# A two-layer diffusion step in fp32: norm rows split by the column factor alone, token factor and shift at eviction, and the low part of the probabilities as the values' last product

## What is computed

```
def rmsnorm(x, g):
    xf = x.astype(F32)
    y = xf * lax.rsqrt(jnp.mean(xf * xf, axis=-1, keepdims=True) + EPS)
    return (y * g.astype(F32)).astype(x.dtype)
...
        sh1, sc1, g1, sh2, sc2, g2 = jnp.split(jax.nn.silu(cond) @ P['mod_w'][i] + P['mod_b'][i],
                                               MOD_CHUNKS, axis=-1)
        h = rmsnorm(x, P['norm1_g'][i]) * (1 + sc1) + sh1
...
        x = x + g1 * y
        h = rmsnorm(x, P['norm2_g'][i]) * (1 + sc2) + sh2
        x = x + g2 * (jnp.square(jax.nn.relu(h @ P['mlp_w1'][i])) @ P['mlp_w2'][i])
```

## Time and profile before

| | us |
|---|---|
| median of 3 runs | 3153.99 |
| lowest, highest | 3151.72, 3156.88 |
| the profiled execution, its own time | 3155.11 |
| span of its trace | 3153.0 |
| granted TensorE clock over the span | 0.968 of full |

### The profile page before, as it was taken

The page is one execution under the profiler, slowest core; times in us unless marked ns, Lnnn a source line. Parts: engine busy times, 40 slices in busy tenths (PEclk is TensorE's granted clock), DMA queues, the critical chain, the costliest instruction groups (busy, mean ns, idle before and its releaser), DMA issues.

```text
span 3153.0 us, 43418 instructions
## 1 busy us (share of the span) xinstructions
PE 3011.7 (96%) x17065; PEld 2884.9 (91%) x17065; DVE 1491.0 (47%) x1825; ACT 1001.6 (32%) x1439; POOL 904.0 (29%) x573
## 2 busy tenths in 40 slices
PE   7999998999999999888999999998989999999999
PEld 7999998999999999787778888786989999999999
DVE  8445546456445554744566655566442222222222
ACT  3111213111111122323777677776222111121111
POOL 0221121112212121122665556666212112222111
PEclk7999998999999999897999999999989999999999
DMA  5222220222212221120000000000201111111112
GB/s 202 96 80 80 80 100 27 81 80 81 70 61 80 80 73 60 53 82 6 8 7 7 2 7 5 8 7 1 100 27 47 41 40 40 47 40 41 40 45 80
DMA packets 45539, 166.69 MB, mean 53 GB/s; under 512 B 5793, under 2 KB 7457, under 8 KB 45217
## 3 DMA queue, kind: packets, MB, share of 16 engines
q1 hardware_dynamic: 44912, 160.89, 15.0%
q10 hardware_dynamic: 560, 4.87, 0.4%
HBM read 156.15 MB, written 9.58 MB: 53 GB/s over the span
## 4 chain that ended last, share of the span: by engine, by line
PE 53%; issue 30%; POOL 14%; DVE 2%; ACT 1%; POOLq 0%; DVEq 0%; ACTq 0%
PE ps L907 52%; POOL p_lo L505 10%; POOL w_lo L489 2%; DVE x L1466 0%; POOL rot L516 0%; POOL q_tok L520 0%; DVE ps L1382 0%; POOL rot L514 0%; PE ps L1002 0%; PE ps L1212 0%; ACT tmp L592 0%; PE ps L996 0%; DVE tmp L1406 0%; POOLq L504 0%; DVE sums L1801 0%
## 5 line engine op out<-in xcount | busy, mean ns | idle before, releaser
L489 POOL TENSOR_TENSOR w_lo<-w_raw,w_hi 128x1024 fp32r<-128x1024 f32 (+2 forms) x190 | 465.2, 2449 | 1884.3 <-ACT w_hi L585 1884.3
L907 PE MATMUL ps<-h_hi,w_hi 128*128 128x384 f32 x2640 | 606.8, 337 | 37.7 <-DVE h_lo L1447 20.2
L907 PE MATMUL ps<-h_lo,w_hi 128*128 128x384 f32 x2640 | 603.3, 336 | 0.0
L907 PE MATMUL ps<-h_hi,w_lo 128*128 128x384 f32 x2640 | 602.6, 336 | 0.0
L907 PEld LDWEIGHTS ps<-h_hi,w_hi 128*128 128x128 f32 x2640 | 473.7, 190 | 42.4 <-issue 29.8
L585 ACT ACTIVATE w_hi<-w_raw 128x1024 fp32r<-128x1024 f32 (+2 forms) x190 | 194.7, 1025 | 956.7 <-PE ps L907 860.9
L907 PEld LDWEIGHTS ps<-h_lo,w_hi 128*128 128x128 f32 x2640 | 474.3, 189 | 0.0
L907 PEld LDWEIGHTS ps<-h_hi,w_lo 128*128 128x128 f32 x2640 | 473.6, 189 | 0.0
L505 POOL TENSOR_TENSOR p_lo<-p,p_hi 128x512 fp32r<-128x512 f32 (+1 forms) x304 | 389.8, 1294 | 257.2 <-ACT p_hi L830 253.3
L1466 DVE SCALAR_TENSOR_TENSOR x<-ps,mod,x 128x256 f32<-128x256 f32 (+5 forms) x432 | 240.2, 612 | 457.9 <-PE ps L907 456.9
L907 PE MATMUL ps<-hid_hi,w_hi 128*128 128x384 f32 x1536 | 348.8, 334 | 0.5 <-DVE x L1466 0.5
(11 more groups left out here) (142 smaller groups left out, 3551.4 us busy)
## 6 DMA issues: line engine op xcount, KB each, us to landing
w_raw<-in_wall_dram SPq DMA_DIRECT2D x174, 512.0 KB, 3.7
mod_raw<-in_mod_rows_dram SPq DMA_DIRECT2D x80, 512.0 KB, 3.6
x<-in_x_t_dram SPq DMA_DIRECT2D x8, 576.0 KB, 8.4
x_spill<-x ACTq DMA_DIRECT2D x1, 4608.0 KB, 13.8
x<-x_spill SPq DMA_DIRECT2D x1, 4608.0 KB, 13.5
out_dram<-x SPq DMA_DIRECT2D x8, 576.0 KB, 2.8
mod_shift<-in_mod_cols_dram SPq DMA_DIRECT2D x8, 512.0 KB, 14.5
mod_scale<-in_scale_rows_dram SPq DMA_DIRECT2D x8, 512.0 KB, 16.6
```

The lines of the kernel that those rows point to most:

```text
L489: pool.tensor_tensor(w_lo[s][:, 0:words], w_raw[s][:, 0:words], w_hi[s][:, 0:words].bitcast(F32), ALU.subtract).then_inc(w_lo_done, 1)
L907: ins = pe.matmul(out, lhs[a], rhs[b](cols), start=first and n == 0, stop=last and n == 2)
```

## The change

**Norms.** h is no longer made ahead of the product. The rows are split from x * gain alone: `h_hi` on ScalarE (`high_tile`, scale = gain), `h_lo` on VectorE (`low_tile`: x * gain - h_hi), already while the last blocks of x are evicted. Two more columns per tile hold the shifts of the two kinds of token (HN = N + 2), so the third matmul of each triple has 386 columns rather than 384 and leaves weights x shift beside the result. The token factor is computed while the first two blocks run: inside `skewed_blocks` TensorE sums the squares at k = 4, spreads eight of nine factor tiles at k = 6 and the last at k = 7. Eviction multiplies by the factor and adds the shift's product.

```
 def skewed_blocks(ready, wide=False):
     for k in range(KT + SKEW):
+        if wide and k == MEAN_AT:
+            norm_means()
+        if wide and k == RMS_AT:
+            norm_broadcast()
+        if wide and k == RMS_AT + 1:
+            norm_last()
...
 # ScalarE, a chunk, k < HT
-act.wait_ge(stage_done, L.count("s", 1))
-act.activation(cols3(tmp[0][:, 0:N]), stage_ps(L.at["s"]), ACT.Relu).then_inc(relu_done, 1)
+if k < HT - 1:
+    split_hi()
 L.at["s"] += 1
 act.wait_ge(stage_free, L.count("s"))
+for a, z, c in SEGS:
+    ins = act.activation(tmp[0][:, a:z], tmp[0][:, a:z], ACT.Relu,
+                         bias=row_shift[:, k % 2, c:c + 1])
+ins.then_inc(relu_done, 1)
+act.wait_ge(relu_done, L.count("hid", -1))
+act.wait_ge(hid_lo_done, L.count("hid"))
+act.activation(tmp[1][:, 0:N], tmp[0][:, 0:N], ACT.Square).then_inc(hid_squared, 1)
+act.wait_ge(hid_squared, L.count("hid", -1))
 act.activation(hid_hi[:, k, :], tmp[1][:, 0:N], ACT.Copy).then_inc(hid_hi_done, 1)
...
 # VectorE, a chunk, k < HT
-dve.scalar_tensor_tensor(cols3(tmp[1][:, 0:N]), stage_ps(L.at["s"]), 0.0,
-                         cols3(tmp[0][:, 0:N]), ALU.max, ALU.mult).then_inc(stage_free, 1)
+dve.tensor_copy(row_shift[:, k % 2, :], shift_row(L.at["s"]))
+dve.tensor_tensor(cols3(tmp[0][:, 0:N]), stage_ps(L.at["s"]), cols3(rstd[:, :]),
+                  ALU.mult).then_inc(stage_free, 1)
...
 # VectorE, the end of out_blocks
+residual(KT - 2, gate + KT - 2)
+add_square(0)
+if mods:
+    mod_next(6 * KT - 1)
+low_shifts(n)
+for j in range(KT // 2):
+    low_tile(n, j)
+residual(KT - 1, gate + KT - 1)
+for j in range(KT // 2, KT - 1):
+    low_tile(n, j)
+add_square(1)
+low_tile(n, KT - 1)
+norm_inverse()
...
 # VectorE, last chunk of layer 0, each half of k >= HT
 residual(j, gate + j)
-if squares:
+if before_norm is not None:
+    if j == 0:
+        low_shifts(before_norm)
     add_square(half)
+    low_tile(before_norm, j)
...
 # ScalarE, latent blocks, behind split_hi of turn k
-if k == QT - 1:
-    act.wait_ge(stage_free, L.at["s"])
-    for j in range(QT):
-        square(ql[:, j, :], j % 2, QR)
+if 1 <= k <= QT:
+    latent_bias(k - 1, ql[:, k - 1, :])
+    square(ql[:, k - 1, :], (k - 1) % 2, QR)
...
+latent_bias(QT + CT, kpe_t[:, :])
 act.wait_ge(stage_done, L.at["s"] - 2)
 latent_high(ql_hi, ql, QT)
```

**Attention.** The values' products change places:

```
-pe.wait_ge(p_lo_done, A.count("j", -1))
-ins = three([(pv_ps(g, slice(0, P), n), 0)], 0, first, last,
-            [r[:, kt, head * VD:head * VD + P] for r in (v_hi, v_lo)],
-            [lambda _, r=r: r[pos % PR][:, 0:n] for r in (p_hi, p_lo)])
-ins.then_inc(p_free, 1)
+pe.wait_ge(p_hi_done, A.count("j", -1))
+pe.matmul(out, v[0], p_hi[s][:, 0:n], start=first, stop=False)
+pe.matmul(out, v[1], p_hi[s][:, 0:n], start=False, stop=False)
 pe.wait_ge(p_lo_done, A.count("j", -1))
+pe.matmul(out, v[0], p_lo[s][:, 0:n], start=False, stop=last).then_inc(p_free, 1)
```

More of the change, by code:

```diff
@@ L572, in _ @@
             L = Place(b=0, s=2, hid=0, acc=0)
-            C = dict(rms=0, t=0)
+            C = dict(rms=0, t=0, norm=0, free=KT - 1, relu=0)
             A = Place(j=0, u=0, r=0, p=0)
@@ L593, in square, with rms @@
                 L.at["acc"] += 1
-            def rms(src, n, width):
-                for j in range(n):
-                    square(src(j), j % 2, width)
+            def rms(out):
                 C["rms"] += 1
@@ L603, in rms, with first_norm @@
                 act.wait_ge(stage_done, L.at["s"] - 1)
-                act.activation(cols3(rstd[:, :]), stage_ps(L.at["s"]), ACT.Copy).then_inc(stage_free, 1)
+                act.activation(cols3(out[:, :]), stage_ps(L.at["s"]), ACT.Copy).then_inc(stage_free, 1)
                 L.at["s"] += 1
[L607 to L611, removed]
+            def first_norm():
                 for j in range(KT):
@@ L658, in mlp @@
                 last = layer == LAYERS - 1
-                chunk(not last, not last)
+                chunk(not last, None if last else 2)
             act.wait_ge(vec_loaded, 16)
@@ L908, in three, with token_tiles, tile_cols, stage @@
                 return ins
-            def stage(w0, tiles, src, ready=None, free=None):
+            def token_tiles(s, wide):
+                v = stage_ps(s)
+                b0 = (3 * (s % 2) + 2) * BANK
+                return [(v[:, 0, :], 0), (v[:, 1, :], 1), (ps[:, b0:b0 + TB + (NC if wide else 0)], 2)]
+            def tile_cols(c, wide):
+                return slice(c * TB, (c + 1) * TB + (NC if wide and c == 2 else 0))
+            def stage(w0, tiles, src, ready=None, free=None, wide=False):
                 s, slot = L.at["s"], L.at["b"] % 2
                 pe.wait_ge(stage_free, L.count("s", 1))
-                v = stage_ps(s)
                 for k in range(tiles):
@@ new lines, in low_tile, with norm_inverse @@
+            def low_tile(n, j):
+                C["h"] += 1
+                dve.wait_ge(h_hi_done, C["h"])
+                for a, z, c in SEGS:
+                    ins = dve.scalar_tensor_tensor(h_lo[:, j, a:z], x[:, j, a:z], gain[:, n, j, c:c + 1],
+                                                   h_hi[:, j, a:z].bitcast(F32), ALU.mult, ALU.subtract)
+                ins.then_inc(h_lo_done, 1)
+            def norm_inverse():
+                C["rms"] += 1
+                dve.wait_ge(mean_root, C["rms"])
+                dve.reciprocal(root[:, :], root[:, :]).then_inc(mean_inverse, 1)
+                C["norm"] += 1
@@ L1471, in out_blocks @@
             def out_blocks(layer, mods):
+                n, gate = 2 * layer + 1, layer * MODS + 2 * KT
+                norm_gain(n)
                 no_squares()
[L1473 removed]
+                with dve.Fori(0, KT // 2 - 1) as i:
                     L.enter(i, s=2, m=2 if mods else 0, acc=2)
```

251 lines of the change are left out of this document (155 added, 96 removed).

## The result

The changed kernel took 3142.15 us in the median of six runs (3136.56 to 3145.25), beside 3155.6 for the kernel before (3151.72 to 3159.08): ratio 0.9956, 95% interval 0.9946 to 0.9966. It is faster by 13.5 us where 29.0 were forecast; the time lies 0.85 us inside the slow end of the range, 3143. The kernel before has six runs here too, hence 3155.6 and not 3153.99. The profiled execution took 3143.97, 11.1 under that of before.

What follows compares the result with a forecast made beforehand. TensorE, busy 96% of the span, was taken as the bound. Terms -20.0 - 20.3 - 7.0 + 9.7 + 2.6 + 6.0 + 1.5 - 1.5 = -29.0 took 3154 to 3125 us; range 3110 to 3143.

Steps and rivals of the forecast that it cites:

- The rows: Rival, chance 0.06, half slower: 4616-byte rows slow TensorE's reads of h in 7920 matmuls, deciding at 3.7 ns each.
- The sign of being wrong, 0.178 us: Matmuls of h taking over 0.178 us in steady blocks would show the forecast wrong.
- under 1 ns: Argument against slower row reads: a row read straight through touches at most one more 16-byte line, costing under 1 ns.
- the hold-ups by weights: Rival, chance 0.10: in skewed pairs low tiles block GpSimd's w_lo, pairs lose 3 to 4 us each: 3136.
- the late hidden tile: Rival, chance 0.10, 0.03 slower: fourth tile's hid_lo overruns its 0.7 us margin at 16 first down-blocks; between, 3130 to 3150.
- the two norms ahead of the MLPs: Mixer's end to third up-block falls to 30.5 us, including 1.2 waiting; gains 20.0 and 20.3 us.
- The norm ahead of the latents: Layer 0's last chunk and pair: period 16.24, pair starts at 1304.3 and ends at 1334.7; gain 7.0 us (4 to 10).
- its second block waits 1.1 us for the eighth residual: In the pair behind layer 0's last chunk, the second block waits 1.1 us, for the eighth residual.
- Latent sums and kpe_t: New stall at the latents' sums, loss 9.7 us (5.2 to 12); kpe_t's product and bias delay attention 2.6 (0 to 2.8).
- The fourth hidden tile: Layer 0's chunks: later split and modulation make TensorE wait 0.85 us for a residual, 6.0 in seven chunks (3.5 to 9).
- Wide columns and attention: Two more columns cost 1.5 us over 70 blocks; attention's later wait for p_lo gains 1.5 us (0 to 10.7).

Runs made afterwards that it cites:

- experiment 1: Kernel before, with only rows of h_hi and h_lo lengthened from 1152 to 1154 words: 3170.77 us beside 3152.07, ratio 1.0057.
- Experiment 8: Changed kernel, with the last weight split of layer 0's last chunk ahead of that block's squares and high tiles: 3138.78 us, ratio to before 0.9946.
- Experiment 6: Changed kernel, with third latent's bias and square ahead of the split waiting for the fourth block, and kpe_t's bias behind ql_hi: 3130.81 us, ratio to before 0.9925.

## Why the prediction was wrong, point by point

- **The rows.** This is the step that failed. The sum put them at nothing; a rival had them, with a chance of 0.06, and was framed as all or nothing: "it decides at 29.0/7920 = 3.7 ns on 174". Measured are 2.2 ns, 17.7 us by the trace and 18.7 by the medians of experiment 1. With them the forecast would have been 3143. The sign of being wrong, 0.178 us, was set at the deciding point too, and 0.1756 passed under it. The trace of before could not show it, but an effect between nothing and the deciding point was the case to price. I set against it the 16-byte lines of the Trainium skill ("SBUF — State Buffer", "Door 1: The DMA port swizzle"). That section gives no price for a new line, so the "under 1 ns" was my own step. No run here bears it out: 1160-word rows, which all begin on such lines, cost 1.4 ns. With 1154 words not "most tiles" start off a line but every second (176.5 ns on average, the others 174.7).
- **Luck.** The time lies in the range only because two rivals, the hold-ups by weights and the late hidden tile, had stretched its slow end to 3143, and neither came as described. That the rows alone lead to 3143 is in part luck too: the 5.7 us missing ahead of the latents (below) and smaller losses were offset by gains that were not forecast, 2.4 at the two norms ahead of the MLPs, 1.3 behind the first and, in this trace, 3.7 in attention.
- **The two norms ahead of the MLPs.** Right: 30.5 forecast, 29.2 measured; the 1.2 of waiting did not come. Third and fourth block gave another 1.3 that the forecast left out: before, the third began behind a wait of 2.90 at half clock (three matmuls in 1.27).
- **The norm ahead of the latents.** 7.0 forecast, 1.3 measured (101.1 to 99.8 from the last chunk's down-blocks to the third latent block). Period (16.10) and start of the pair (1302.69 against 1304.3) were right. The pair was priced at 1.1 of waiting and 30.4 in all; it waited 4.02 for w_lo, ran at a granted clock of 0.88 and took 38.0. The step "its second block waits 1.1 us for the eighth residual" overlooked that on ScalarE the split stood behind that residual's square and high tile. Experiment 8 shows it: with the split ahead, the wait is gone and the pair takes 31.3.
- **What GpSimd does to low tiles.** The rival "held up by weights" had the right resource: 1.54 us became 3.69. By the Trainium skill ("SBUF — State Buffer", "Who interferes with whom") whichever of the two instructions starts first has the pair of ports for its whole length. The trace agrees: the piece of 128 columns, 0.35 us alone, took 2.49 beside a low part of 2.56. It cost the last chunk little, since the modulation's product, once 3.43, ran free behind it. In the pairs behind the mixers, where the rival looked, one piece of 1024 columns took 2.54 and 3.10 us in place of 1.28, and TensorE did not wait for it.
- **Latent sums and kpe_t.** 9.7 and 2.6 forecast, 9.1 and 2.6 measured. Experiment 6 gave 8.3 and 2.7 back.
- **The fourth hidden tile.** The wait of 0.85 is exact; with the restart behind it it cost 1.14 a chunk, 8.0 and not 6.0.
- **Wide columns and attention.** Four up-blocks are 0.80 us longer, 0.64 with the row length alone, so the two columns cost 0.16, an estimate of 2.8 us over 70 blocks where 1.5 was forecast. For attention 1.5 was forecast; about 2.7 is likely and not settled.
- **The first 54 us.** Counted from TensorE's first matmul, the first of h came at 51.3 to 54.9 us in executions of the changed kernel and its variants, which have the same code there; 2.8 us that the trace of the changed kernel lost lie here.

## What to carry to other kernels

A layout change is a change of every reader: two words more in a row cost each of the 7920 matmuls that read it 2.2 ns, in code that the change did not touch. Look for such readers, count them, and price a few nanoseconds each even where no row shows any.

Where a step is hoisted out of a serial chain, follow each in-order queue that it enters: the two biggest stalls, 8.3 us at the latents' sums and 4.7 in the pair ahead of them, were each a weight split on the wrong side of a square.

## What the hardware showed unexpectedly

A matmul of 128x384 whose moving rows are 4608 bytes apart took 173.33 ns at three placements; with 4616 bytes it took 175.56 and with 4640 bytes 174.72 on average. With 4640 bytes ten or eleven matmuls right behind the sums ran at half clock in both layers of both kernels that have such rows, without a pause ahead.

While GpSimd made a low part, a VectorE instruction of 128 columns with two operands in SBUF took 2.49 us in place of 0.35 (the changed kernel), and one of two columns 2.18 in place of 0.23 (the kernel of experiment 8):

```profile
1300.79 2.41 POOL L511 TENSOR_TENSOR w_lo<-w_raw,w_hi 128x1024 fp32r<-128x1024 f32 x1 [2.21 <-ACT w_hi L607]
...
1301.04 2.18 DVE L1498 TENSOR_SCALAR mod<-mod_acc,mod_bias 128x2 f32<-128x2 f32 x1
```
